# Fewer unread matmuls around the delta-rule grams and the latent attention of a hybrid encoder

## The reference, cut to what matters

```python
def even_mixer(u, pos, ...):
    proj = u @ w_in
    qkv, conv_new = causal_conv(conv0, proj[..., :GDN_QKV], conv_w)
    ...
    o, s_new = gated_delta(q, k, v, beta, g, s0)          # chunks of 64 tokens
    ...
    o_mla = mla_attend(q_nope, q_rope, pos, k_nope, k_rope, v, k_pos)
    out = jnp.concatenate([o_gdn, o_mla], axis=-1) @ w_out

def gdn_chunk_step(s0, inp):
    lower = jnp.where(strict, beta[..., :, None] * decay * jnp.einsum('bhtd,bhsd->bhts', k, k), 0.0)
    sol = lax.linalg.triangular_solve(lower + jnp.eye(C), rhs, lower=True, unit_diagonal=True)
    u = sol[..., :dv] - jnp.einsum('bhtk,bhkv->bhtv', sol[..., dv:], s0)
    o = gam * (q @ s0) + ((q @ k.T) * decay) @ u
    s_new = jnp.exp(g_end) * s0 + (jnp.exp(g_end - G) * k).T @ u

def mla_block(q_nope, q_rope, q_pos, k_nope, k_rope, v, k_pos):
    s = (q_nope @ k_nope + q_rope @ k_rope) * MLA_SCALE
    p = softmax(where(visible, s, -inf))
    return p @ v
```

## Time and profile before

| | |
|---|---|
| median of 3 runs | 2555.35 us (2549.14 to 2561.02) |
| the profiled execution's own time | 2571.54 us |
| its span, first to last instruction | 2569.9 us |
| PE busy | 2466.7 us, 96% |
| DVE busy | 1453.2 us, 57% |
| ACT busy | 722.2 us, 28% |
| mean granted TensorE clock | 0.98 |

### The profile page before, as it was taken

One profiled execution on the slowest core, in us unless ns is written; L12 is line 12 of the kernel. 1 busy time (PEld: TensorE's weight loads), 2 busy tenths in 40 slices (PEclk: granted clock), 3 DMA queues, 4 the chain that ended last, 5 costly groups with the idle time before them and its releaser, 6 DMA issues.

```text
span 2569.9 us, 41177 instructions
## 1 busy us (share of the span) xinstructions
PE 2466.7 (96%) x18104; PEld 2366.9 (92%) x18104; DVE 1453.2 (57%) x2311; ACT 722.2 (28%) x1002; POOL 142.5 (6%) x215
## 2 busy tenths in 40 slices
PE   6999999999899989999999999999989999999996
PEld 6999999998787668999999999999968989999995
DVE  4767765574563435864465686677667455333323
ACT  3211121444333324311121521221255243111212
POOL 2000000200000001100000200000000010000001
PEclk9999999999997889999999999999989999999998
DMA  6445542122000012443343154333324122222221
GB/s 281 150 161 185 183 166 96 64 90 49 13 1 17 27 66 74 159 162 116 122 164 121 61 180 156 111 144 145 140 74 138 58 74 83 78 83 86 83 72 48
DMA packets 55873, 275.09 MB, mean 107 GB/s; under 512 B 7216, under 2 KB 17008, under 8 KB 33040
## 3 DMA queue, kind: packets, MB, share of 16 engines
q1 hardware_dynamic: 38304, 177.43, 19.7%
q0 software_dynamic: 15952, 91.73, 10.1%
q10 hardware_dynamic: 1440, 3.32, 0.4%
HBM read 259.13 MB, written 13.32 MB: 106 GB/s over the span
## 4 chain that ended last, share of the span: by engine, by line
PE 66%; DVE 5%; ACT 1%; issue 1%; DMA 0%; POOL 0%; SPq 0%; DVEq 0%; ACTq 0%
PE ps L273 50%; PE ps L280 4%; PE ps L497 2%; PE ps L480 2%; DVE x L599 1%; PE ps L291 1%; PE ps L1200 1%; PE ps L1209 1%; DVE ln_rstd_tail L595 1%; PE ps L1635 1%; PE ps L1213 0%; PE ps L2338 0%; PE ps L1429 0%; PE ps L1634 0%; PE ps L1420 0%
## 5 line engine op out<-in xcount | busy, mean ns | idle before, releaser
L273 PE MATMUL ps<-u_hi,w_hi 128*128 128x288 f32 x3040 | 653.2, 296 | 2.1 <-DVE w_lo L265 1.2
L273 PE MATMUL ps<-u_hi,w_lo 128*128 128x288 f32 x3040 | 650.3, 296 | 0.0
L273 PE MATMUL ps<-u_lo,w_hi 128*128 128x288 f32 x3040 | 650.3, 296 | 0.0
L265 DVE TENSOR_TENSOR w_lo<-w_raw,w_hi 128x2048 fp32r<-128x2048 f32 (+3 forms) x184 | 360.6, 1960 | 350.0 <-ACT w_hi L257 346.3
L257 ACT ACTIVATE w_hi<-w_raw 128x2048 fp32r<-128x2048 f32 (+3 forms) x184 | 303.5, 1649 | 888.8 <-DMA w_raw<-in_w_in 420.1
L273 PEld LDWEIGHTS ps<-u_hi,w_hi 128*128 128x128 f32 x3040 | 490.7, 189 | 6.8 <-issue 3.5
L273 PEld LDWEIGHTS ps<-u_lo,w_hi 128*128 128x128 f32 x3040 | 490.5, 189 | 0.0
L273 PEld LDWEIGHTS ps<-u_hi,w_lo 128*128 128x128 f32 x3040 | 490.1, 189 | 0.0
L621 DVE SCALAR_TENSOR_TENSOR ada_out<-ada_w,c_act 128x1024 f32<-128x1024 f32 x272 | 317.0, 1221 | 28.8 <-DMA ada_w<-in_w_ada 26.9
L273 PE MATMUL ps<-h_lo,w_hi 128*128 128x288 f32 x1392 | 293.4, 295 | 0.0
L273 PE MATMUL ps<-h_hi,w_hi 128*128 128x288 f32 x1296 | 280.9, 298 | 0.0
(11 more groups left out here) (384 smaller groups left out, 2604.0 us busy)
## 6 DMA issues: line engine op xcount, KB each, us to landing
w_raw<-in_w_in SPq DMA_DIRECT2D x88, 1024.0 KB, 4.8
ada_w<-in_w_ada POOLq DMA_DIRECT2D x64, 1024.0 KB, 4.9
w_raw<-in_w_out SPq DMA_DIRECT2D x32, 768.0 KB, 4.4
w_raw<-in_w_out SPq DMA_DIRECT2D x32, 640.0 KB, 3.8
w_raw<-in_w_mix_in SPq DMA_DIRECT2D x10, 1024.0 KB, 4.9
ada_w<-in_w_ada SPq DMA_DIRECT2D x8, 1024.0 KB, 26.1
output_matrices<-wm_new POOLq DMA_DIRECT2D x8, 576.0 KB, 3.1
wm<-output_matrices POOLq DMA_DIRECT2D x8, 576.0 KB, 4.4
```

What stands on the lines that cost most here:

```text
L265: dve.tensor_tensor(w_lo[:, g % NS, 0:WIDTH[g]], w_raw[:, g % NS, 0:WIDTH[g]], w_hi[:, g % NS, 0:WIDTH[g]].bitcast(F32), ALU.subtract).the ...
L273: m = pe.matmul(out[:, a, :], w, mv[:, a, :], start=start and n_ == 0, stop=stop and n_ == 2)
```

## The change

The six unread matmuls at the end of each gram go (five grams, 30 matmuls). The 14 ahead of the attention go, and with them the wait for the first rotated query pair that stood before them; the wait for all three rotations stays. In the first ten turns of the attention loop one unread matmul stands in place of three (20 fewer). 64 of the 102 go; those of the single block's levels and of the last chunk's scan stay.

```diff
                 for h in range(HEADS):
                     m = pe.transpose(bank(i_, n_)[:, h, :], f(h), ident[:, :])
                 m.then_inc(s_g1[w], 1)
-            keep_warm(pe, 7, 6)
...
             mm.then_inc(s_rp, 1)
-        pe.wait_ge(s_kr, 1)
-        keep_warm(pe, 0, 14)
         pe.wait_ge(s_kr, 3)
         for n in range(NU + 2):
...
             if n < 10:
-                keep_warm(pe, 6, 3)
+                keep_warm(pe, 6, 1)
```

## The result

| | before | after |
|---|---|---|
| median of the first runs | 2552.24 us (4 runs) | 2587.05 us (4 runs, 2568.49 to 2589.94) |
| median of a second series, run later | 2558.45 us (35 runs, 2542.90 to 2582.20) | 2582.65 us (12 runs, 2549.68 to 2600.21) |
| profiled execution's own time | 2571.54 us | 2589.94 us |
| its span | 2569.9 us | 2588.3 us |

The account below looks back on a forecast made before the run. PE, busy 96% of the span, was taken to bound the kernel, locally where others wait for it and by its clock. -1.3 + 1 + 20 + 2.5 = +22 us: median from 2555.35 to 2577, range 2556 to 2592.

Parts of the forecast that it names:

- The grams of the pairs: Two pairs' grams: removal gains 0.6 us in each first block, nothing in the second; -1.3 us taken.
- The +1 for a fall behind the longer pause: Behind each pair's grams: PE's pause grows to some 3 us and may drop the clock to 0.50; +1 us for both.
- The single block: Single block's gram and levels: clock falls near 778 to 781, levels take 12.1 us in place of 6.55; +20 us.
- The attention: Attention's first ten turns: scores start at the low clock, thinner turns climb back some 7 us later; +2.5 us.
- The four first turns: Start of the attention: 10.0 us to unit 4 against 10.06 before, less work at a worse clock.
- rival 3: Low clock in single block and in attention until the units of 512 keys: +30 us, 2585, up to 2592; chance 0.14.
- doesn't climb back by itself: Single block's stage: once at the low clock it stays there until the dense products behind it lift it.
- the stage's price is the same at either: Whole stage: same cost in the profiled execution and the median run, so the median goes from 2555.35 to 2577 us.
- Rival 1: Single block: clock holds in the levels, 6.5 us each; -1.3 + 2.5, 2557 us, not slower; chance 0.25.
- Rival 2: All 64 removed matmuls were on PE's path and the clock doesn't care: 15.7 us gained, 2540 us; chance 0.03.

Follow-up runs that it names:

- pairs_gone: Kernel before without the 24 unread matmuls of the four 128-token grams: median 2545.05 us against 2552.05, ratio 0.9990.
- after_again: The changed kernel, unedited, run again with more runs: median 2582.65 us against 2558.45 for the kernel before, ratio 1.0023.
- fourteen_gone: Kernel before without the 14 unread matmuls ahead of the attention and their wait, three a turn kept: one profiled execution, attention 74.6 us.
- single_gone: Kernel before without the six unread matmuls of the single block's gram: median 2552.97 us against 2552.05, ratio 1.0038.
- attention_only: Kernel before with only the attention's edits, the 14 gone and one in place of three in ten turns: 2552.34 us against 2552.05, ratio 1.0001.
- the thin ones: Kernel before with the single block's six unread matmuls on 64 columns in place of 512: 2583.76 us against 2558.45, ratio 1.0059.
- all_gone: Changed kernel without the 38 unread matmuls it keeps, so none at all: 2578.09 us against 2558.45 for the kernel before, ratio 1.0066.
- six_moved: Kernel before with the single block's six unread matmuls behind its first product in place of ahead: 2559.62 us against 2560.38, ratio 0.9994.

## Why the prediction was right, and where it was not

Its working was against the profiled execution, so its terms are compared there.

- **The grams of the pairs**, -1.3: measured -0.7 and -0.7, sum -1.4. The cover is as described, DVE in the second block, and only DVE's wait in the first is gained. The +1 for a fall behind the longer pause was 0 in this execution. In `pairs_gone` it came and cost about 2 us in the first pair and nothing in the second. In `after_again` low stretches of 3.4 and 6.8 us lie behind the grams and cost nothing: its pair 1 took 55.5 because the clock was still low when it began, and the first gram took 8.5 us in place of 6.5. A term of +1 for something that costs 0 or about 2 was fair.
- **The single block**, +20: 74.9 - 54.1 = +20.8. A level was priced at 12.1 us and took 11.9. That the sum fits to 0.8 us is luck: both sides are draws. The same code of the single block took 44.8 to 55.6 us in other profiles with the six, and 55.6 in `after_again` without, so the difference could have come out anywhere from 0 to +30. The place is near, and partly luck as well: the fall was named for 778 to 781 and came at 780.94, but the gram began 5.3 us later in this execution than before. By the gram's own start it was named for 5 to 8 us behind and came after 2.45, inside the gram and ahead of where the six had stood.
- **The attention**, +2.5: 76.0 - 72.3 = +3.7. The four first turns, forecast as 10.0, took 10.4. The low clock held until 917.47, in the units of 256 keys as said, but for 13 us of them and not 7 (904.52 to 917.47). The reason given, that thinner turns climb more slowly, is borne out by `fourteen_gone`: with three a turn the clock was back after 10.0 us in place of 23.
- **Not in the sum**: the products between were 2.6 us faster (low clock for 6.0 us there in place of 11.5, the tails of the long stretches counted), and 2.0 us less outside the stage. All in all +18.4 on the span, against +22. The median of the first series moved by +34.8, to 2587.05: that is inside the range, above the 2569 to 2584 that the prediction named as the forecast's own, and among the times of rival 3, whose mechanism the trace doesn't show.

The step that failed, though the time came out inside the range, is the claim that at the low level the stage "doesn't climb back by itself", and with it that "the stage's price is the same at either" execution. In `single_gone` and `after_again` it climbed back after 23.9 us, inside the levels, and then the last chunk ran fast as well: about 56 us, as much as the kernel before with its late fall. And the kernel before doesn't always have that late fall: the same code in `pairs_gone` and `attention_only` took 44.8. So the change doesn't add 20 us; it moves the executions from a piece of 45 to 57 us to one of 56 to 75. That is a part of why its runs reach from 2550 to 2600, and why the first four, three of them near 2588, gave +35 us and the next twelve +24; another part is the pace of the dense products (last section).

Rival 1 (the clock holds in the levels) was not seen in any profile of a kernel without the six: five of five fell, counting the thin ones. But its time, within some 10 us of the kernel before, came up in 4 of 12 runs. Whether by a fall that ends early isn't shown: the profiled execution in which it did took 2578 us. Rival 2, all 64 on PE's path, is out by the pieces of `pairs_gone` and by the 4.93 us that PE now waits for `kr`. Rival 3 (low clock in both stages, until the units of 512 keys) was not seen in the changed kernel; `all_gone` came near it, low until 921.71, in the units of 384 keys.

The Trainium skill, "TensorE: Matmul & The Clock Gate", section "Loop structure matters more than you think", names a long wait for DMA as what costs the clock and a copy by DVE as harmless. Around the gram no DMA is waited for, the pauses are those of ACT and DVE, and the measurement decides against the rule: `single_gone` and `after_again` fell behind pauses for DVE of 0.96 to 1.35 us, and the changed kernel behind one of 1.27 us for ACT. Its section "What's actually happening" says that the low clock is the default and activity lifts it. The trace agrees that the low clock is what a stage can stay in, but a busy PE alone didn't lift it: in `all_gone` it stayed at 0.50 through 64.9 us, 61.3 of them busy, on small products.

What stays open: what decides in an execution whether the clock comes back after 24 us or after 75. The program is the same. In the five profiles the two whose fall came behind the gram climbed back and the three whose fall came inside it stayed low; five executions don't make that a cause.

## What to carry to other kernels

An unread matmul had two prices here, and both are read off the timeline: its own time, which is nothing where the next instruction waits for another engine, and the clock of everything behind it. Before taking one out, look at what PE has left in that stretch and how small the work is that follows. Ahead of the single block's small products the clock that PE enters with was worth up to 30 us (44.8 against 74.9), and the six matmuls take 1.5. Judge such an edit by the spread of many runs and by the pieces of the stage, since one profile or four runs show one draw.

## What the runs showed that was not expected

The dense products of the feed-forwards run at one of two paces at the same granted clock of 1.00. The windows of the kernel before, then of the changed one, over two stretches of 300 us (the first at one pace in both, the second not):

```profile
100.00:400.00 300.00, 300.00 (x2253) 300.00 (x2252) 212.02 (x305) 56.05 (x43) 13.71 (x26) 1.00 0.48 171
1050.00:1350.00 300.00, 300.00 (x2253) 300.00 (x2252) 181.20 (x249) 56.23 (x43) 9.52 (x18) 1.00 0.41 147
```

```profile
100.00:400.00 300.00, 300.00 (x2252) 300.00 (x2251) 214.01 (x309) 56.90 (x43) 13.71 (x26) 1.00 0.49 169
1050.00:1350.00 300.00, 299.72 (x2300) 299.26 (x2300) 195.35 (x272) 67.84 (x62) 16.30 (x25) 1.00 0.41 144
```

2253 matmuls in 300 us are 133.2 ns each, 2300 are 130.4 and 2310, where a whole stretch keeps the faster pace, 129.9, with the same instructions. A feed-forward keeps its pace for some 350 us, which makes about 9 us (an estimate, 350 x 3.3 / 133.2); the four of them draw apart from each other. By that estimate the whole program can vary by some 30 us for a reason that the granted clock doesn't show. Two profiles show the ends: `single_gone` has 2310 matmuls in 300 us in all four, and its span without the stage is 2248.7 us; `six_moved` has 2252 in all four, and 2291.2 us. That is of the size of the spread of the kernel before (2531 to 2570 us in 31 runs), and so 2 to 5 us of this stage can't be told by timing. It is also why `single_gone`, low for 23.9 us, has the shortest span of all the profiles. What sets the pace was not tried.
